# A decoder layer's last stretch, rearranged: attention projection per token tile, eight experts picked first, last chunks row by row

## What is computed

```python
y_a = attn @ w_attn_out                                  # attention output, 16 heads x 64
y_b = conformer_conv(...) @ w_conv_out
y = jax.nn.sigmoid(g_a) * y_a + jax.nn.sigmoid(g_b) * y_b     # merge
y = y @ w_out
x = x + gt1 * rmsnorm(y, g_post_mix)                     # first norm
h = rmsnorm(x, g_pre_ffn) * (1.0 + sc2) + sh2            # second norm
q = (h @ w_q).reshape(T, PEER_HEADS, 2, PEER_DQ // 2)    # 8 heads x 2 x 128
s = jnp.einsum('thcd,hckd->thck', q, sub_keys)           # 128 scores per head and half
s1, i1 = lax.top_k(s[:, :, 0], 16)
s2, i2 = lax.top_k(s[:, :, 1], 16)
cand = s1[..., :, None] + s2[..., None, :]               # 16 x 16 candidates
top_s, pos = lax.top_k(cand, 16)                         # 16 experts per head
act = gelu(einsum('cd,ced->ce', hc, u[ec]))              # 128 experts per token
y = einsum('ce,ced->cd', act * softmax(top_s), v[ec])
x = x + gt2 * rmsnorm(y, g_post_ffn)
```

## Time and profile before

| what | value |
|---|---|
| median of 3 runs | 1099.29 us |
| profiled execution, its own time | 1102.63 us |
| its span | 1100.9 us |
| TensorE busy | 952.5 us (87%) |
| VectorE busy | 727.8 us (66%) |
| ScalarE busy | 280.6 us (25%) |
| bytes moved | 363.46 MB, mean 330 GB/s |
| gathers (queue q0 holds them) | 292.59 MB, 65.2% of the 16 engines' span |

### The profile page before, as it was taken

The page is one execution under the profiler, slowest core; times in us unless marked ns, Lnnn a source line. Parts: engine busy times, 40 slices in busy tenths (PEclk is TensorE's granted clock), DMA queues, the critical chain, the costliest instruction groups (busy, mean ns, idle before and its releaser), DMA issues.

```text
span 1100.9 us, 10654 instructions
## 1 busy us (share of the span) xinstructions
PE 952.5 (87%) x3151; PEld 568.0 (52%) x3151; DVE 727.8 (66%) x1901; ACT 280.6 (25%) x770; POOL 330.9 (30%) x324
## 2 busy tenths in 40 slices
PE   5999999999999998899879987886677678777786
PEld 4888888878645856655445443332233233333332
DVE  6699798724563127667667677677677667767553
ACT  2111122226564012431222231221331221221212
POOL 0101003021000004254335454454444454455410
PEclk9999999999999998899999999999989999899989
DMA  9967749886103535999999999999999999999992
GB/s 364 403 242 215 264 154 351 337 292 111 58 1 104 165 115 223 422 421 423 421 423 423 423 423 424 421 423 424 422 424 423 423 422 423 424 422 423 424 422 88
DMA packets 63559, 363.46 MB, mean 330 GB/s; under 512 B 7515, under 2 KB 8171, under 8 KB 30476
## 3 DMA queue, kind: packets, MB, share of 16 engines
q0 software_dynamic: 43136, 292.59, 65.2%
q1 hardware_dynamic: 20364, 70.18, 17.7%
HBM read 361.15 MB, written 1.59 MB: 329 GB/s over the span
## 4 chain that ended last, share of the span: by engine, by line
PE 54%; DMA 36%; DVE 5%; ACT 2%; POOL 2%; issue 1%; SPq 0%; ACTq 0%; DVEq 0%; POOLq 0%
DMA pair<-in_peer_uv,idx 29%; PE pb L486 21%; PE pb L712 16%; DMA arena<-in_peer_uv,idx 4%; PE pb L501 3%; PE pb L607 2%; PE pb L637 2%; DMA ring<-in_peer_uv,idx 2%; PE pb L517 1%; PE pb L650 1%; PE pb L691 1%; DVE pair L1318 1%; PE pb L737 1%; POOL arena L456 1%; PE pb L620 1%
## 5 line engine op out<-in xcount | busy, mean ns | idle before, releaser
L712 PE MATMUL pb<-arena,sig 128*128 128x512 f32 x432 | 210.9, 641 | 64.8 <-ACT sig L941 64.7
L456 POOL DMA_INDIRECT arena<-in_peer_uv,idx x108 | 130.2, 1206 | 236.5 <-PE pb L712 165.8
L486 PE MATMUL pb<-hT,ring 128*128 128x256 f32 x880 | 190.7, 379 | 0.5 <-ACT arena L796 0.5
L486 PEld LDWEIGHTS pb<-hT,ring 128*128 128x128 f32 x880 | 167.0, 190 | 25.1 <-ACT arena L796 1.7
L712 PEld LDWEIGHTS pb<-arena,sig 128*128 128x128 f32 x432 | 86.3, 206 | 180.6 <-issue 180.3
L1318 DVE CUSTOM_DVE_ANT_0 arena<-arena,sig 128x1024 f32<-128x1024 f32 x108 | 130.9, 1227 | 73.3 <-DMA arena<-in_peer_uv,idx 72.6
L712 PE MATMUL pb<-ring,sig 128*128 128x512 f32 x224 | 106.5, 621 | 23.1 <-ACT sig L941 23.1
L938 ACT ACTIVATE gl<-dot 128x4 f32<-128x4 f32 (+1 forms) x67 | 13.7, 205 | 442.0 <-DVE dot L1318 425.7
L1065 DVE SCALAR_TENSOR_TENSOR y<-arena,cols,y x240 | 95.2, 476 | 0.0
L1318 DVE CUSTOM_DVE_ANT_0 ring<-ring,sig 128x1024 f32<-128x1024 f32 x56 | 67.7, 1224 | 29.7 <-DMA ring<-in_peer_uv,idx 29.4
L712 PEld LDWEIGHTS pb<-ring,sig 128*128 128x128 f32 x224 | 43.5, 198 | 83.4 <-issue 83.4
(11 more groups left out here) (228 smaller groups left out, 1212.4 us busy)
## 6 DMA issues: line engine op xcount, KB each, us to landing
ring<-in_w_stream SPq DMA_DIRECT2D x103, 512.0 KB, 6.7
arena<-in_w_ada POOLq DMA_DIRECT2D x32, 512.0 KB, 11.2
arena<-in_w_ada SPq DMA_DIRECT2D x12, 512.0 KB, 13.4
arena<-in_w1k SPq DMA_DIRECT2D x8, 512.0 KB, 9.0
sig<-in_w_ada SPq DMA_DIRECT2D x4, 512.0 KB, 15.3
arena<-in_w1v POOLq DMA_DIRECT2D x1, 2048.0 KB, 7.8
arena<-rev_scratch POOLq DMA_DIRECT2D x16, 128.0 KB, 6.8
arena<-in_peer_uv,idx POOLq DMA_INDIRECT x108, 26.8
```

Source lines behind the costliest of these rows:

```text
L456: nc.gpsimd.indirect_dma_start(out=rowat[PLACE[n]], out_offset=None, in_=a["peer_uv"], in_offset=bass.IndirectOffsetOnAxis(ap=idx[:, c, e: ...
L486: last = mm(pb[:, bank, 0:SEQ], w[:, k * P:(k + 1) * P], src[:, k, :], start=(k == 0), stop=(k == DT - 1))
L712: last = mm(pb[:, 4 + 2 * t + hf, :], diag[:, c % DEEP, e, :], rowat[PLACE[n]][:, D + hf * 512:D + (hf + 1) * 512], start=(i == 0 and e == ...
```

## The change

1. **Convolution projection.** All six column tiles that were spread or left over (2 to 7) are spread over the first 16 attention units, three matmuls in most units where there were two. The two that stood after unit 31 are gone from there.
2. **Attention projection per token tile.** `attention_out_half(t, j)` makes 128 columns at a time. Tile 0's eight halves and its output projection come first; tile 1's halves follow, and all of tile 1's output projection comes after them.
3. **Eight experts first.** `first_unit` picks the best 8 of head 0's candidates from the best 8 x 8, sets `v_first`, on which gather 0 waits, and then does the rest.
4. **First chunk early.** VectorE takes the dots of chunk 0 before `token_norms(1)`, ScalarE does its exp, gelu and diagonals before `out_norm(1)` (with the table of Sqrt loaded again in between), and TensorE does chunk 0 before steps 4 and 5. Unit 1 is retrieved around chunks 0 and 1, unit 2 around 2 and 3.
5. **Places.** The 12 places are taken in another order, in which places come free for gathers 0 and 1, then 2 to 5, 6 and 7, 8 to 11. Eight tiles of `w_out` and some of `w_q` get buffers of their own, and the fourth broadcast row (`rows_load(3)`) is loaded at gather 84, where the 16 places begin (before: 92).
6. **Steps.** 22 instead of 20; 7 of them before chunk 1, then one per chunk (before: one per two chunks).
7. **Last three chunks** row by row instead of the last one.

```diff
-CO_FIRST, CO_LAST = 2, 6
-CO_PER = 2
+CO_FIRST = 2
+CO_UNITS = [(j, ks) for j in range(CO_FIRST, DT)
+            for ks in ((range(0, 4), range(4, 8)) if j % 3 == 1 else (range(0, 3), range(3, 6), range(6, 8)))]
...
-SOON, SLOTS, LATE = 12, 16, 92
-OUT_FREE, QUERY_FREE = 10, 11
-STEPS = [(m, (0,)) for m in range(4)] + [(m, (1,)) for m in range(4)] + [(m, (0, 1)) for m in range(4, 2 * PH)]
-EARLY = 10
+SOON, SLOTS, LATE = 12, 16, 84
+ATTN_FREE, MERGED_FREE, OUT_FREE = 2, 6, 8
+STEPS = [(m, (0,)) for m in range(6)]
+for _m in (0, 2, 4):
+    STEPS += [(_m, (1,)), (_m + 1, (1,)), (_m + 6, (0, 1)), (_m + 7, (0, 1))]
+STEPS += [(m, (0, 1)) for m in range(12, 2 * PH)]
+EARLY = 7
+LAST = 3
...
-    return [(s, s + 1) for s in range(CH)] if c == TT * CPT - 1 else [(0, CH)]
+    return [(s, s + 1) for s in range(CH)] if c >= TT * CPT - LAST else [(0, CH)]
...
+                if n == T_WQ + 5:
+                    sp.wait_ge(ring_used, T_WQ)
...
-            g.wait_ge(v_mx, 2 * NU)
-            g.wait_ge(v_m, DT)
+            g.wait_ge(p_t, NU)
...
+                if n == 0:
+                    g.wait_ge(v_first, 1)
+                elif n == 8:
+                    g.wait_ge(v_idx, 1)
+                elif n % (SEG * CH) == 0:
                     g.wait_ge(v_idx, n // (SEG * CH) + 1)
+                if n == ATTN_FREE:
+                    g.wait_ge(ring_used, T_OUT)
+                if n == MERGED_FREE:
+                    g.wait_ge(v_m, TT * DT // 2)
                 if n == OUT_FREE:
                     g.wait_ge(ring_used, T_WQ)
...
+            def attention_out_half(t, j):
+                tile = T_AO + j
...
+                for k in range(DT):
+                    last = mm(pb[:, MERGE_BANK[q], side * P:(side + 1) * P], tile_at[SLOT[tile]][:, k * P:(k + 1) * P],
+                              hT[:, k, t * P:(t + 1) * P], start=(k == 0), stop=(k == DT - 1))
...
+            unit_exp(0)
+            gelu_next()
+            coefficients(0)
+            fn(turned[:, :], eps[:, :], ACT.Sqrt).then_inc(a_turn, 1)
             out_norm(1)
...
+            first_unit()
+            merged(DT - 2)
+            merged(DT - 1)
+            expert_dots(0)
+            token_norms(1)
+            retrieve(1, 0)
+            for c in range(1, TT * CPT):
+                k, b = divmod(c, SEG)
+                expert_dots(c)
+                if c == 1:
+                    retrieve(1, 1)
+                    retrieve(1, 2)
```

More of the change, by code:

```diff
@@ L128, with used @@
 SLOT, TURN, PRIOR = tile_places()
+def used(n):
+    return n + 1 if n < T_WQ else T_WQ + 1 + WQ_ORDER.index(n - T_WQ)
+OUT_BANK = (2, 6)
+MERGE_BANK = [4, 0, 1, 5] + [4, 5] * 2
+MERGE_BANK_BEFORE = [max((q for q in range(n) if MERGE_BANK[q] == MERGE_BANK[n]), default=-1)
+                     for n in range(TT * DT // 2)]
 def landed(n):
@@ L640, in values @@
                         last.then_inc(p_o, 1)
+            def attention_out_half(t, j):
+                tile = T_AO + j
+                if t == 0:
+                    pe.wait_ge(ring_in[SLOT[tile]], 16 * TURN[tile])
+                q, side = divmod(t * DT + j, 2)
+                if side == 0 and MERGE_BANK_BEFORE[q] >= 0:
+                    pe.wait_ge(v_m, MERGE_BANK_BEFORE[q] + 1)
+                for k in range(DT):
+                    last = mm(pb[:, MERGE_BANK[q], side * P:(side + 1) * P], tile_at[SLOT[tile]][:, k * P:(k + 1) * P],
+                              hT[:, k, t * P:(t + 1) * P], start=(k == 0), stop=(k == DT - 1))
+                last.then_inc(ring_used if t else p_ao, 1)
             def conv_pieces(n):
-                for p in range(n * CO_PER, (n + 1) * CO_PER):
-                    j, k = CO_FIRST + p // DT, p % DT
-                    if j >= CO_LAST:
-                        return
+                j, ks = CO_UNITS[n] if n < len(CO_UNITS) else (DT, ())
+                for k in ks:
                     if k == 0:
@@ L752, in _ @@
             subkey_scores(1)
-            for k in range(4, DT):
+            for j in range(4, DT):
+                attention_out_half(1, j)
+            for k in range(DT):
                 out_part(1, k).then_inc(ring_used, 1)
@@ new lines, in _, with decode @@
+            eights = onehs[0][:, :, 0:8, 0:8]
+            def decode(lo, shift, mask, one, n, width):
+                ps = slice(lo, lo + n)
+                ch.add(V_.tensor_single_scalar(pa[:, 0, ps], p16[:, ps], shift, ALU.logical_shift_right))
+                ch.link(V_.tensor_single_scalar(pa[:, 1, ps], p16[:, ps], mask, ALU.bitwise_and))
+                ch.link(V_.tensor_copy(paf[:, :, ps], pa[:, :, ps]))
+                ch.link(V_.tensor_tensor(one, iota16[:, 0:width].unsqueeze(1).unsqueeze(1).broadcast_to((P, 2, n, width)),
+                                         paf[:, :, ps].unsqueeze(3).broadcast_to((P, 2, n, width)), ALU.is_equal))
+                ch.link(V_.tensor_tensor(one, one, i16f[:, :, 0:width].unsqueeze(2).broadcast_to((P, 2, n, width)),
+                                         ALU.mult))
+                ch.link(V_.tensor_reduce(e12[:, :, ps], one, AX, ALU.add))
+                V_.scalar_tensor_tensor(out=idx[:, 0:SEG, :].rearrange("p a b -> p (a b)")[:, ps],
+                                        in0=e12[:, 0, ps], scalar=float(NK), in1=e12[:, 1, ps],
+                                        op0=ALU.mult, op1=ALU.add).then_inc(v_idx if lo else v_first, 1)
@@ new lines, in _, with finish_tile @@
+            dve.wait_ge(g_const, 4)
+            def finish_tile(t):
+                dve.wait_ge(rows_in, 64)
+                dve.wait_ge(a_ss, 3 * TT + t + 1)
+                ch.link(V_.tensor_tensor(scaled[1], pb[:, 4 + 2 * t:6 + 2 * t, :].rearrange("p a b -> p (a b)"),
+                                         rows[3], ALU.mult))
+                dve.wait_ge(a_std, 6 + t)
+                ch.link(V_.reciprocal(rstd[:, 6 + t:7 + t], std[:, 6 + t:7 + t]))
+                for hf in range(2):
+                    cs = slice(hf * 512, (hf + 1) * 512)
+                    V_.scalar_tensor_tensor(out=x[:, t, cs], in0=scaled[1][:, cs], scalar=rstd[:, 6 + t:7 + t],
+                                            in1=x[:, t, cs], op0=ALU.mult, op1=ALU.add).then_inc(v_out, 1)
+                dve.wait_ge(v_out, 2 * (t + 1))
@@ new lines, in _ @@
+            first_unit()
[4 more added lines that the diff above has]
+            retrieve(1, 0)
+            for c in range(1, TT * CPT):
+                k, b = divmod(c, SEG)
[3 more added lines that the diff above has]
+                    retrieve(1, 2)
+                elif c == 2:
+                    retrieve(2, 0)
+                    retrieve(2, 1)
+                elif c == 3:
+                    retrieve(2, 2)
+                elif b and k + 2 < UNITS:
```

270 lines of the change are left out of this document (156 added, 114 removed).

## The result

The changed kernel took 1093.66 us (median of 6 runs, 1091.43 to 1094.51) beside 1100.29 us of the kernel before in the same comparison (6 runs, 1098.77 to 1102.01). The ratio is 0.9925, 95% interval 0.9910 to 0.9939: faster by about 8 us (0.75%), against 10.4 forecast. The two medians themselves differ by 6.6 us, which is the low edge of that interval. 1093.66 lies in the range 1081 to 1096 and 4.7 us above the 1089 named. Two later comparisons gave 0.9921 (0.9907 to 0.9934) and 0.9927 (0.9909 to 0.9945), with medians 8.8 and 8.2 us apart. In the second of them one of the six executions of the changed kernel took 4513.53 us in a slow state; no ratio counts it, and without it that kernel's median is 1093.63 us instead of 1093.80.

A forecast was written before the change was run, and what follows sets the result against it. It took a compute chain up to about 428 us, then 256 gathers at full DMA rate, as the bound. 16.8 - 5.0 - 1.2 - 4.3 + 4.1 = 10.4 us off 1099.29 gave 1088.9, rounded 1089; range 1081 to 1096.

The forecast's parts named there:

- rival A: The forecast itself: an earlier start, a small hole in the gather queue, a short tail; 1084 to 1093 us, chance 0.60.
- B: Early start mostly eaten: queue holes of 8 to 12 us up to chunk 17; 1093 to 1096 us, chance 0.15.
- first gather, all in all: Chain from the attention to the first gather: gather 0 goes at 409.0 us, 16.8 us earlier.
- convolution pieces in the units: First 16 attention units: 32 more matmul records on a fully busy TensorE cost 6.9 us, bounds 0 to 6.9.
- five loads in the full stage: Transfers after gathers start: four w_q tiles cost 5.0 us and the fourth broadcast row 1.2 us.
- hole before gather 16: Gather queue: DMA engines idle while gather 16 waits for unit 1's indices; costs 4.3 us, bounds 0 to 10.
- tail by rows: Last three chunks: TensorE has no backlog and finishes 1.7 us after the last diagonal; gains 4.1 us, bounds 0 and 4.5.
- a rule against the change: Tail: idle gaps between rows may drop TensorE to the lower clock, 3.4 instead of 1.7 us for the last row; 1091.
- C: Better: convolution pieces hide partly in the attention and the hole closes; gain 14.7 to 21.6 us, 1078 to 1084, chance 0.10.
- E: Chain's end: working by rows does nothing there, so the 4.1 us go; 1093 us, chance 0.09.
- 10.8 against 11.2 per chunk: Full stage: TensorE needs 10.8 us per chunk against the queue's 11.2, staying narrowly under it to chunk 17.
- D: Slower: chunk 0 ahead of the second norms delays unit 1 if row 3 lands late; hole 19.7 us, 1104, chance 0.06.

The follow-up runs named there:

- extra: Changed kernel with six added loads of 0.5 MB each, put between gathers 100 and 180; 1099.79 us, ratio 0.9971 to the kernel before.
- last1: Changed kernel with only the last chunk by rows instead of the last three; 1096.06 us, ratio 0.9951 to the kernel before.
- idx16: Changed kernel with VectorE doing the whole second retrieval before the dots of chunk 1; 1089.40 us, ratio 0.9890 to the kernel before.
- places: Changed kernel with the third and fifth w_q tiles given other places, to load before the first gather; 1088.06 us, ratio 0.9860 to the kernel before.
- b_last3: Kernel before with its last three chunks by rows instead of the last one; 1099.89 us, ratio 0.9969 to the kernel before.

## Why the prediction was right, and what it missized

The course is that of rival A, the forecast: an earlier start, a small hole, a shorter tail. The time is not quite: 1093.66 is just above A's 1084 to 1093, in the stretch named for B. The traces exclude B, so it is A with terms that came out smaller. Term by term, from unit 0, in us gained:

| term | predicted | measured |
|---|---|---|
| first gather, all in all | 16.8 | 16.0 |
| (in it: convolution pieces in the units) | (-6.9) | (-9.6) |
| five loads in the full stage | -6.2 | -5 to -6, by extra's loads in mid-queue |
| hole before gather 16 | -4.3 | -3.4 |
| tail by rows | +4.1 | +3.7, of which 1.5 a low clock in before's profile |
| sum | 10.4 | 9.5 in the traces, about 8 by the ratio |

The measured terms add up to 10 to 11, 1 to 2 us more than the traces' 9.5. Which term takes that is not shown.

**The convolution's pieces are the term that was off.** The matmuls cost what they cost elsewhere: six records take 1.30 us at L702 and a whole tile took 3.65 behind unit 31, so 32 take 6.9 to 7.3. Another 2.0 are the two waits for VectorE. Reading the density from a window that is 100% busy gave the work, not the dependences that the new grouping makes.

That the sum held in spite of it was luck. Four steps behind it were each 0.5 us quicker than I took them: the output product of tile 0 was done 34.7 us after unit 31 (35.2 said), four halves took 7.2 (7.7), transposes to first scores 6.5 (7.0), and the first eight indices came 3.7 us after MAX8 (4.2). These 2.0 us offset most of the 2.7 that the pieces cost more.

**The loads.** Of the five, the broadcast row was loaded at 360.85 in the kernel before, ahead of the first gather, and at gather 84 in the changed one; the "before: 92" of the change's fifth point is only where its 16 places begin. So it is an added load of the full stage, as the prediction has it.

**Tail.** 4.1 was read from one execution whose TensorE had the lower clock for some microseconds (the earlier trace rows has its row: 0.50 in 1080 to 1082, and I used it only for a rule against the change, not for the price of the tail before). At full clock the rows are worth 2.2 in the trace of last1; the medians say 3.1 and 2.8.

**The median.** 10.4 was taken from 1099.29, the median of three runs. With six it was 1100.29, and in three later comparisons the kernel before stood at 1101.7, 1102.7 and 1102.0. In the first comparison 1.0 us is the base and 3.8 us are 10.4 against the medians' 6.6; together they are the 4.7 us between 1089 and 1093.66.

**Chances.** A, C, E and four fifths of B add up to 0.91 and not to the 0.88 named, and what is left for "within 0.3%" is 0.03 and not 0.06.

**Rivals.** B: there is no hole between 470 us and the tail, although TensorE has 95.91 of 100 us busy in 500 to 600; the narrow 10.8 against 11.2 per chunk held. C: the pieces hide nowhere; but its second half, the hole closed, is what idx16 and places come near to. D: from unit 0 row 3's dot was 2.7 us after the forecast landing, not 15, and ScalarE began tile 1's norm at 430.50, before the 435 set as the sign. E: refuted by last1 and b_last3. The table load took 1.28 us in the changed kernel too (429.10), and the next ACTIVATE starts right behind it (430.39). The 2.7 us of the Trainium skill (ScalarE: Activation LUTs, Table sets: the hidden batching unit) is not seen; the same page makes it up of about 1283 ns for the load, which agrees with the trace, and a drain of about 1380 ns, which does not show here.

What I had not weighed at all: the three tiles among the first rows. The prediction counts them at 3.7 us of queue and in row 3's landing; it doesn't ask whether they could load in the idle stretch before. places shows 5.4 us for two of them, nearly as much as the largest loss in the sum.

## What to carry to other kernels

In this kernel a load that was issued just as the first rows of the gather queue were waited for cost twice, its own transfer and the delay of whoever waited for the row behind it. Look for such loads, and find them a place that is free during an idle stretch. An earlier start of a stage that the transfers bound is worth the idle time it removes, not the time by which it is earlier. When a wait is moved in front of other work, look at which engine's list it blocks: VectorE stood idle 6.5 us ahead of the very work whose lateness made the hole.
